# Transposing x before its norm in a hybrid attention block on one Trainium2 core

## The reference

```python
def rms_norm(x, gain):
    y = x * lax.rsqrt(jnp.mean(x * x, axis=-1, keepdims=True) + EPS)
    return y * gain

h = rms_norm(x, attn_norm)
proj = h @ w_in                      # 1024 x 3352
nq, nkc, nvc, nks, nvs, nkw, nvw, ngate, hq, hf, hi, hg = split(proj)
y_nsa = nsa_mixer(...)               # q and k get a norm per head, then rope
y_nsa = rms_norm(y_nsa, nsa_out_norm)
# hgrn2: silu(hq), sigmoid(hf) -> decay f, k = 1 - f, value hi; a state over chunks
o = rms_norm(o, hgrn_out_norm) * silu(hg)        # per head of 128
x = x + concat([y_nsa, o]) @ w_out
h = rms_norm(x, mlp_norm)
x = x + jnp.square(relu(h @ w_mlp_in)) @ w_mlp_out
```

## Time and profile before

| What | us |
|---|---|
| Median of 3 runs (1619.61 to 1621.15) | 1621.14 |
| The profiled execution, its own time | 1615.88 |
| Its span, first to last instruction | 1614.1 |
| First product of block 0 | 47.45 |
| Copies out of block 4 begin | 243.65 |
| State phase ends, unit 0 begins | 800.98 |
| Last adds begin | 1606.26 |

### The profile page before, as it was taken

The page is one execution under the profiler, slowest core; times in us unless marked ns, Lnnn a source line. Parts: engine busy times, 40 slices in busy tenths (PEclk is TensorE's granted clock), DMA queues, the critical chain, the costliest instruction groups (busy, mean ns, idle before and its releaser), DMA issues.

```text
span 1614.1 us, 23957 instructions
## 1 busy us (share of the span) xinstructions
PE 1526.2 (95%) x8325; PEld 1306.0 (81%) x8333; DVE 745.8 (46%) x1344; ACT 391.2 (24%) x833; POOL 411.8 (26%) x419
## 2 busy tenths in 40 slices
PE   2999998997999999989979999999999999999998
PEld 2888887886888888889968888888888888888886
DVE  3100862006657676779763454334443344444334
ACT  5111413115444545441410421100111001111110
POOL 1333422321000000000323073333334444433411
PEclk9899999999999999999989999999999999999999
DMA  4212121200000000012111021111111111111102
GB/s 154 53 46 52 46 70 47 52 2 4 2 0 0 0 0 0 0 40 105 39 41 52 1 91 40 46 46 45 45 52 52 52 52 52 45 45 52 48 18 104
DMA packets 45967, 68.43 MB, mean 42 GB/s; under 512 B 7352, under 2 KB 25184, under 8 KB 45920
## 3 DMA queue, kind: packets, MB, share of 16 engines
q1 hardware_dynamic: 41936, 66.93, 13.5%
q10 hardware_dynamic: 3984, 0.85, 0.3%
HBM read 63.57 MB, written 4.19 MB: 42 GB/s over the span
## 4 chain that ended last, share of the span: by engine, by line
PE 88%; DVE 7%; ACT 2%; issue 2%; ACTq 1%; DVEq 0%
PE ps L428 65%; PE ps L1587 7%; PE ps L1547 4%; PE ps L1562 4%; PE ps L1610 3%; PE ps L1581 1%; PE ps L1445 1%; PE ps L1531 1%; PE ps L637 1%; DVE hgrn_vg L1313 1%; PE ps L1552 1%; DVE x L1403 1%; DVE hT_low L487 0%; DVE hgrn_A L1280 0%; DVE normed_rows L1052 0%
## 5 line engine op out<-in xcount | busy, mean ns | idle before, releaser
L781 POOL CAST w_high<-w_raw 128x512 fp32r<-128x512 f32 x144 | 101.6, 705 | 659.4 <-PE ps L428 383.8
L1403 DVE SCALAR_TENSOR_TENSOR x<-ps,rsqrt_t,x 128x512 f32<-128x512 f32 x256 | 177.4, 747 | 91.9 <-PE ps L428 91.9
L428 PE MATMUL ps<-w_high,hidden_high 128*128 128x512 f32 x512 | 199.4, 390 | 1.7 <-DVE x L1403 1.7
L428 PE MATMUL ps<-x1T_high,w_high 128*128 128x512 f32 x512 | 199.3, 389 | 0.0
L428 PE MATMUL ps<-w_low,hidden_high 128*128 128x512 f32 x512 | 199.2, 389 | 0.0
L428 PE MATMUL ps<-w_high,hidden_low 128*128 128x512 f32 x512 | 199.2, 389 | 0.0
L428 PE MATMUL ps<-x1T_high,w_low 128*128 128x512 f32 x512 | 199.2, 389 | 0.0
L428 PE MATMUL ps<-x1T_low,w_high 128*128 128x512 f32 x512 | 199.2, 389 | 0.0
L783 POOL TENSOR_TENSOR w_low<-w_raw,w_high 128x512 fp32r<-128x512 f32 x144 | 195.2, 1356 | 11.5
L1384 DVE TENSOR_TENSOR relu_squared<-relu 128x512 f32<-128x512 f32 x60 | 47.1, 809 | 294.0 <-ACT relu L1033 293.7
L428 PE MATMUL ps<-w_high,hT_high 128*128 128x512 f32 (+1 forms) x448 | 170.6, 381 | 2.4 <-DVE hT_low L487 1.4
(11 more groups left out here) (188 smaller groups left out, 2341.5 us busy)
## 6 DMA issues: line engine op xcount, KB each, us to landing
w_raw<-in_w_mlp_in_dram SPq DMA_DIRECT2D x64, 256.0 KB, 2.7
w_raw<-in_w_mlp_out_dram SPq DMA_DIRECT2D x64, 256.0 KB, 2.8
w_raw<-in_w_in_dram SPq DMA_DIRECT2D x48, 256.0 KB, 2.7
x_in<-in_x_dram SPq DMA_DIRECT2D x8, 512.0 KB, 8.7
w_raw<-in_w_out_dram SPq DMA_DIRECT2D x16, 256.0 KB, 2.8
x<-in_x_dram SPq DMA_DIRECT2D x8, 512.0 KB, 7.3
out_dram<-x SPq DMA_DIRECT2D x8, 512.0 KB, 3.6
w_raw<-in_w_in_dram SPq DMA_DIRECT2D x8, 140.0 KB, 7.2
```

The costliest lines, as they stand in the source:

```text
L428: ins = nc.tensor.matmul(out_ap, a_hl[i], b_hl[j], start=first and n == 0, stop=last and n == 2)
L781: pool.tensor_copy(high[:, j, :], w_raw[:, j, :]).then_inc(w_highs, 1)
L1403: dve.scalar_tensor_tensor(xs, ps[:, (0 if g == 2 else 4) + tt, :], rs_t[:, 48 + t:49 + t], xs, ALU.mult, ALU.add)\
```

## The change

Four edits.

1. **Raw x is transposed.** PE transposes `x_in` itself, tile by tile as it lands; bank k collects feature block k of four tiles. ACT's copy out multiplies by the gain, one number for a partition (`gcol`, `attn_gain_columns`), and DVE's low part likewise. The squares and the factors of the rows are made on ACT and DVE behind these copies. The two constants that are needed first, the eye and `gcol`, are issued first and have a semaphore of their own (`e_loaded`). `gcol` is 128 x 8 single elements; the broadcast `gain_row` of 512 KB is gone. SP issues the first four chunks of `w_in` between x tiles 5 and 6.
2. **The factors act at the copies out.** ACT's `evacuate` has them as its scale. Blocks 3 and 4 have tokens along the free axis. For them PE transposes the factors into two banks within block 1, DVE copies these to `R`, and DVE copies blocks 3 and 4 out, multiplied by `R` (`scaled_features`); ACT's Silu and Sigmoid run then in place. DVE does two of the eight tiles of `head_rows` ahead of block 3's copies and six between those and block 4's.
3. **Four output chunks normed in the state phase.** ACT and DVE make the factors of tiles 0 to 3 in the state phase at chunk 5, and DVE norms tiles 0 to 3 there and just after.
4. **Half-row stores.** Each tile is stored in two halves of its row, the left ones as soon as they are added.

```diff
             for t in range(NT):
+                if t == 6:
+                    for j in range(RING):
+                        load_chunk(sp, 0, j, w_in0[j * P:(j + 1) * P, 2 * BW:NSAW], TAIL, first=True)
                 sp.dma_start(x_in[:, t, :], x[0, t * P:(t + 1) * P, :]).then_inc(x_loaded[t], 16)
...
-            for t in range(NT):
-                sp.wait_ge(res_out, added(NFB) - NT + t + 1)
-                sp.dma_start(out[0, t * P:(t + 1) * P, :], x1[:, t, :]).then_inc(out_sent, 16)
-            sp.wait_ge(out_sent, 16 * NT)
+            for half in range(2):
+                for t in range(NT):
+                    sp.wait_ge(res_out, added(NFB) - 2 * NT + NT * half + t + 1)
+                    cols = slice(half * BW, (half + 1) * BW)
+                    sp.dma_start(out[0, t * P:(t + 1) * P, cols], x1[:, t, cols]).then_inc(out_sent, 16)
+            sp.wait_ge(out_sent, 32 * NT)
...
-            for g in range(2):
-                for t in range(4 * g, 4 * g + 4):
-                    act.wait_ge(x_loaded[t], 16)
-                    act.activation(junk[:, t % 2, :], x_in[:, t, :], ACT.Square, accum_out=ssq[:, t:t + 1])\
-                        .then_inc(sums_ready, 1)
-                    act.wait_ge(sums_ready, t + 1)
-                root_act(act, cols_of(4 * g, 4 * g + 4), D)
...
+            act.wait_ge(e_loaded, 32)
+            for tg in range(2):
+                for k in range(KC):
+                    act.wait_ge(rowsT_done, KC * tg + k + 1)
+                    act.activation(HT_H[:, k, tg * BW:(tg + 1) * BW], ps[:, k, :], ACT.Copy, scale=gcol[:, k:k + 1])\
+                        .then_inc(rows_high, 1)
+            for t in range(NT):
+                act.wait_ge(x_loaded[t], 16)
...
+            root_act(act, cols_of(0, NT), D)
+            act.wait_ge(norm_step, 5)
...
             for c in range(NT):
                 out_act(act, c)
+                if c == 5:
+                    act.wait_ge(osum_ready, 4)
+                    root_act(act, cols_of(NT, NT + 4 * HH), P)
                 if c in (4, 5):
                     fill_act(act, Y_AT + 4 * (c - 4), 4, mixed_at(HT_H, 0, c - 4), y_gain)
-                if c == 6:
-                    act.wait_ge(osum_ready, 4)
-                    root_act(act, cols_of(NT, NT + 4 * HH), P)
...
+            head_rows(0, EARLY_ROWS)
+            scaled_features(0)
+            head_rows(EARLY_ROWS, NT - EARLY_ROWS)
             dve.tensor_copy(qg[:, 0:1], qg[:, 0:1]).then_inc(prep_done, 1)
+            scaled_features(1)
...
                 state(c)
                 if c:
                     output_sums(c - 1)
+                if c == 5:
+                    root_dve(dve, cols_of(NT, NT + 4 * HH), P)
+                    out_rows(0)
+            for t in range(1, 3):
+                out_rows(t)
             output_sums(NT - 2)
-            root_dve(dve, cols_of(NT, NT + 4 * HH), P)
-            for t in range(4):
-                dve.wait_ge(ho_out, t + 1)
-                out_rows(t)
+            out_rows(3)
             output_sums(NT - 1)
...
-            pe.wait_ge(c_loaded, 16 * NCONST)
+            pe.wait_ge(e_loaded, 32)
             for t in range(NT):
-                transpose_rows(pe, 0, t, row)
+                pe.wait_ge(x_loaded[t], 16)
+                for k in range(KC):
+                    if t == 4:
+                        pe.wait_ge(rows_low, k + 1)
+                    ins = nc.tensor.transpose(ps[:, k, (t % 4) * P:(t % 4 + 1) * P], x_in[:, t, k * P:(k + 1) * P], eye[:])
+                    if t % 4 == 3:
+                        ins.then_inc(rowsT_done, 1)
...
-            pe.wait_ge(rows_low, 2 * NT)
             for j in range(KC):
-                rows_chunk(pe, 0, j, TAIL, proj_full)
+                rows_chunk(pe, 0, j, TAIL, proj_full, lambda b: pe.wait_ge(rows_low, KC + b + 1))
...
+                    if blk == 1 and b == 2:
+                        pe.wait_ge(proj_out, 8)
+                        pe.wait_ge(norm_step, 5)
+                        for t in range(NT):
+                            ins = nc.tensor.transpose(ps[:, 6 + t // 4, (t % 4) * P:(t % 4 + 1) * P],
+                                                      rstd[:, t:t + 1].to_broadcast([P, P]), eye[:])
+                            if t % 4 == 3:
+                                ins.then_inc(R_full, 1)
+                    if blk == 1 and b >= 6:
+                        pe.wait_ge(R_out, b - 5)
```

More of the change, by code:

```diff
@@ L235, in program @@
     x_in = sb("x_in", [P, NT, D], F32, NSA_AT)
[L236 to L237 removed]
+    R = sb("row_roots_as_rows", [P, S], F32, HV_AT + 24832)
     junk = sb("squares", [P, 2, D], F32, FM_AT + 12288)
@@ L292, in program @@
     g2col = sb("mlp_gain_columns", [P, KC], F32)
+    gcol = sb("attn_gain_columns", [P, KC], F32)
     unused = sb("unused", [P, 1], F32)
@@ L314, in program @@
     c_loaded = sem("constants_loaded")
+    e_loaded = sem("eye_and_attn_gain_loaded")
+    R_full = sem("row_roots_transposed")
+    R_out = sem("row_roots_out")
+    fm_done = sem("feature_rows_done")
     pool_set = sem("pool_set")
@@ L1047, in _, with scaled_features @@
         def _(dve):
[L1048 to L1060 removed]
+            dve.wait_ge(e_loaded, 32)
+            for tg in range(2):
+                for k in range(KC):
+                    dve.wait_ge(rows_high, KC * tg + k + 1)
+                    high = HT_H[:, k, tg * BW:(tg + 1) * BW]
+                    dve.scalar_tensor_tensor(HT_L[:, k, tg * BW:(tg + 1) * BW], ps[:, k, :], gcol[:, k:k + 1], high.bitcast(F32),
+                                             ALU.mult, ALU.subtract).then_inc(rows_low, 1)
+            root_dve(dve, cols_of(0, NT), D)
+            for half in range(2):
+                dve.wait_ge(R_full, half + 1)
+                dve.tensor_copy(R[:, half * BW:(half + 1) * BW], ps[:, 6 + half, :]).then_inc(R_out, 1)
+            def scaled_features(i):
+                for b in range(8):
+                    c, half = divmod(b, 2)
+                    if b < 7:
+                        dve.wait_ge(proj_full, (i + 3) * 7 + b + 1)
+                    else:
+                        dve.wait_ge(w_used, (i + 4) * KC)
+                    dve.tensor_tensor(fm[:, i, 4 * half:4 * half + 4, c, :], ps[:, b, :].rearrange("p (c t) -> p c t", t=P),
+                                      R[:, half * BW:(half + 1) * BW].rearrange("p (c t) -> p c t", t=P), ALU.mult)\
+                        .then_inc(proj_out, 1)
+            dve.wait_ge(c_loaded, 16 * NCONST)
             for t in range(NT):
@@ L1459, in compress_pe, with freed_rows, wait @@
                 pe.wait_ge(cmp_out, 3)
-            pe.wait_ge(rows_low, 2 * NT)
             for j in range(KC):
-                rows_chunk(pe, 0, j, TAIL, proj_full)
+                rows_chunk(pe, 0, j, TAIL, proj_full, lambda b: pe.wait_ge(rows_low, KC + b + 1))
+            def freed_rows(blk):
+                def wait(b):
+                    pe.wait_ge(proj_out, (blk - 1) * 8 + (b + 1))
+                    if blk == 1 and b == 2:
[8 more added lines that the diff above has]
+                        pe.wait_ge(R_out, b - 5)
+                return wait
+            for blk in (1, 2):
+                for j in range(KC):
+                    rows_chunk(pe, blk * KC, j, BW, proj_full, freed_rows(blk))
             def freed(blk):
                 return lambda b: pe.wait_ge(proj_out, (blk - 1) * 8 + (b + 1))
-            for pair in range(3):
+            for pair in range(1, 3):
                 if pair == 2:
```

144 lines of the change are left out of this document (55 added, 89 removed).

## The result

| | us | runs |
|---|---|---|
| Before, on the same chip | 1620.94 | 5 (1613.65 to 1621.15) |
| Changed | 1605.39 | 5 (1604.82 to 1608.06) |
| Ratio | 0.9912 | 95% interval 0.9895 to 0.9928 |

A forecast was written before the change was run, and what follows sets the result against it. PE, 88% of the last-ending chain, was taken as the bound. Terms -21.3 + 1.0 + 1.0 - 2.7 - 2.1 = -24.1 us took 1621.1 to 1597.0 us, with an 8-in-10 range of 1590 to 1604.

The forecast's parts named there:

- The front: Start to block 0's first chunk: its end moves from 52.4 to 31.1 us, a gain of 21.3 us.
- I take the early end, since it is second on its queue: Front: gain column lands about 3.6 us after issue; the upper bound was 20.6 us.
- ACT must be done with issuing its 15 loads, as before: Front: ACT's last issue at 9.96 + 2.58 us, first work at 13.97 us, both unchanged.
- gain column late: Front rival: gain column lands late and delays PE's first transposes, giving 1600 to 1609 us; chance 0.12.
- R: Block 1: eight more PE transposes to make the factor tile, +1.0 us, with 2.0 as upper end.
- Blocks 3 and 4: DVE copies these blocks out, running slightly late and delaying prep_done and the compression: +1.0 us, from 0.5 to 3.
- The doubt from "SBUF — State Buffer": Blocks 3 and 4: if DVE and POOL lock each other out, copies take 1.24 times as long, costing 2.2 us.
- The state phase: Unit 0 starts 6 us late, but PE doesn't wait for DVE in unit 1: -2.7 us, from -4.5 to 0.
- the forecast's own better end: State phase: -4.5 us if PE's clock isn't lost during its longer wait.
- Stores: End of kernel: half-row stores build no queue, so the last lands at 1611.5 us: -2.1 us (-1.8 to -2.5).
- The base: Profiled execution 1615.88 us, median 5.3 us above it; the same distance was assumed for the changed kernel.

The follow-up runs named there:

- e5: Changed kernel plus 64 unused DVE semaphore increments before the key copies, gain loaded as 8 rows and transposed by PE: 1594.61 us, ratio 0.9844.
- e1: Changed kernel plus 64 semaphore increments nobody waits for, on DVE ahead of its copies of the keys: 1597.61 us, ratio 0.986.
- e2: Changed kernel plus 128 semaphore increments nobody waits for, on DVE ahead of its copies of the keys: 1605.93 us, ratio 0.9924.
- e4: Kernel before plus 37 semaphore increments nobody waits for, on DVE ahead of its copies of the keys: 1628.64 us, ratio 1.0057.
- e10: Kernel before plus 128 semaphore increments nobody waits for, on DVE ahead of its copies of the keys: 1620.45 us, ratio 1.0006.
- e12: The changed kernel run and profiled once more, with nothing altered: 1606.75 us, ratio 0.9922.
- e14: Kernel before plus 25 unused PE transposes in the gaps between transposes of keys ahead of the attention: 1616.42 us, ratio 0.9982.

## Why the prediction was off

- **The front: the chain right, the column's landing and ACT's readiness wrong.** Forecast -21.3, measured -17.6 against the first profile and -15.6 against the second (at its block 0 the first had the lower clock, and the second, which started at the same time, the higher). The step "I take the early end, since it is second on its queue" failed: the column landed 11.1 us after issue, not 3.6. So did "ACT must be done with issuing its 15 loads, as before": it was done at 15.0 us and not 12.6. With the rows of e5 in the column's place it was done at 14.06, so only part of that is the stall behind the column. The rival "gain column late" was this case, and its arithmetic was right (12.36 + 25 x 0.228 = 18.06 us, measured 18.05); I gave it 0.12. The Trainium skill ("DMA: Bandwidth & Descriptors", section on queues and rings) led me to expect no long wait between single elements and x's pieces. The trace doesn't bear this out: 424 packets of one queue stand against 425 of the other. The 1024 elements took 11.1 us to land while x was loading, and e5's 8 rows were there by 5.56, less than 4.4 after issue.
- **R: right** (+1.0 forecast, 0.9 measured). **Blocks 3 and 4: +1.0 forecast, about 0.1 measured.** The six tiles of heads took 5.9 us each ((224.08 - 188.8) / 6) and not 6.42; DVE was in time and `prep_done` too. The doubt from "SBUF — State Buffer" of the Trainium skill did not come about: the copies with R took 5.45 us for eight, as ACT's 5.36 before, and each of the sixteen 0.69 us, though POOL worked for 1.98 us beside those of block 3 and not at all beside those of block 4.
- **The attention: the missing step.** The sum had nothing there, for the reason that no line of it was changed; this is the step that failed most. It cost 9.1 us against the second profile of before, more than the whole miss of 8.4. e1, e2, e4 and e10 show why: 37 instructions more ahead of DVE's loop.
- **The state phase: mechanism right in each point, size too small.** Unit 0 6.2 us late (forecast 6), no wait in unit 1; 4.3 us gained where 2.7 were forecast. The clock was back by 803 us, which was the forecast's own better end (-4.5).
- **Stores: right**, -2.6 for -2.1.
- **The base.** The profiled execution was 5.3 us below its median, and I moved the sum over by that distance. Part of the distance, 3.0 us, lay in one place, the low clock ahead of the attention, as the second profile shows. It did not change the forecast.

Forecast against measured, from the second profile of before: front 5.7 us worse, attention 9.1 worse, blocks 1.1, state phase to last adds 2.4 and stores 0.5 better, and 1.7 better between the attention and hgrn_A (48.8 against 50.5 us; the changed kernel's second profile, e12, took 51.5 there with the clock low for 6.8 us and not 3.4, so it differs between executions with the clock). That is 9.1 us; in medians it is 8.4. Without the fetches the changed kernel runs in 1597.6 us, the time that was forecast; but this is partly chance, as a front 4 to 6 us worse stands against a state phase, stores and blocks together 4 us better. The range was too narrow at its upper end, since it held no case for code that isn't touched.

## What to carry to other kernels

When an edit adds or removes instructions on an engine ahead of a loop, look at the instruction queues of the DMA view in the loop's later trips: if packets move there, shift the loop by some tens of instructions and measure again. Loads of single elements don't belong ahead of the first work beside large loads, nor do issues of what is needed only later. And before a profiled execution serves as a base, take a second one and compare stretches: here one program's stretch ahead of the attention differed by 3 us through the clock.

## What was not expected of the hardware

- A loop of 296 instructions on DVE is fetched once or anew in each trip, depending on where it begins: shifts of 37 (on before) and 0 and 128 (on the changed kernel) fetched anew, 64 on the changed kernel and 0 and 128 on before did not. It costs 8.5 to 9.4 us over three trips (337.3 against 328.8 us, and the means of all profiles). Where exactly the border lies was not tried.
- The late instruction costs 1.6 to 2.2 us, the trip about 3: the rest is PE's clock, low for 35 us of the attention in the mean and not for 24. Low stretches begin at the same place with the short wait too (e1).
- While both load, the queue of SP and that of ACT move packets one for one (425 and 424 in 4 us), 4 KB against 4 bytes.
- 25 transposes that nobody reads, 3.6 us of PE's time in its waits, came with medians about 3 us lower in three kernels (for e14 the ratio's interval ends at 0.9999). In one of the three profiles the clock fell at the attention's entry all the same.
- 64 semaphore increments on a waiting chain cost 3.2 us themselves and 5.3 in all.
